# First expert place built by one-hot products from the residual tiles, router logits from unnormalised rows, router and experts in one block, room gathers issued at place 7

## The reference

```
x   = x + concat(NA, RWKV, MEM) @ W_out
x   = x + HierMoE(RMSNorm(x))

def rms_norm(x, w):
    y = xf * lax.rsqrt(jnp.mean(xf * xf, axis=-1, keepdims=True) + RMS_EPS)
    return y * w
def hierarchical_moe(h, ...):
    glogits = h2 @ w_group + b_group            # 4 groups, argmax
    elogits = h2 @ w_expert + b_expert          # 16 experts, top 2 inside the group
    ... weights = g_w[:, None] * top_p
    # for every expert: its tokens' rows xb = h2[toks]
    hid = jax.nn.silu(xb @ w_gate[e]) * (xb @ w_up[e])
    out = (hid @ w_down[e]) * wts[:, None]      # added to the token's row
```

## Time and profile before

| | us |
|---|---|
| median of 3 runs | 1241.48 (1239.05 to 1243.29) |
| the profiled execution | 1245.58 |
| its span in the trace | 1243.9 |
| PE busy in the span | 1159.4 |
| DVE busy | 558.1 |
| ACT busy | 307.5 |
| POOL busy | 213.7 |
| mean granted TensorE clock | 0.971 of full speed |

### The profile page before, as it was taken

How to read it: one execution, slowest core, us unless ns; L and a number is a source line. 1 busy time by engine, 2 the same in 40 slices (tenths; PEclk the granted TensorE clock), 3 DMA queues, 4 the chain that set the end, 5 groups by cost and what they waited for, 6 DMA issues and landing times. The chain is left out here.

```text
span 1243.9 us, 24829 instructions
## 1 busy us (share of the span) xinstructions
PE 1159.4 (93%) x10130; PEld 654.0 (53%) x10130; DVE 558.1 (45%) x1345; ACT 307.5 (25%) x791; POOL 213.7 (17%) x260
## 2 busy tenths in 40 slices
PE   5999999999999888899999999749999999899996
PEld 5534444444444566699995455524444444455553
DVE  4448536899695554555773344634111111111111
ACT  5154114432220666633441222200000000000000
POOL 0200410110000324200000001241345511112211
PEclk9989999999999899999999999869999999999998
DMA  9311422151301833234424831557999989667433
GB/s 325 98 42 39 156 79 67 34 177 48 113 17 53 188 77 109 71 86 115 125 58 170 323 120 69 199 230 286 366 359 339 379 326 368 229 254 279 135 123 108
DMA packets 104988, 209.57 MB, mean 168 GB/s; under 512 B 35509, under 2 KB 70805, under 8 KB 100777
## 3 DMA queue, kind: packets, MB, share of 16 engines
q1 hardware_dynamic: 79688, 129.28, 30.2%
q0 software_dynamic: 17264, 47.22, 11.4%
q10 hardware_dynamic: 7920, 31.46, 7.5%
HBM read 178.75 MB, written 35.58 MB: 172 GB/s over the span
## 5 line engine op out<-in xcount | busy, mean ns | idle before, releaser
L522 PE MATMUL pj_ps<-hT,pj_w 128*128 128x512 f32 x576 | 254.1, 597 | 0.0
L522 PEld LDWEIGHTS pj_ps<-hT,pj_w 128*128 128x128 f32 x576 | 108.3, 191 | 136.0 <-issue 135.5
L2197 PE MATMUL ex_py<-wd,ex_hT 128*128 128x512 f32 x256 | 115.2, 601 | 0.0
L1404 PE MATMUL ps_out<-w_out,mixT 128*128 128x512 f32 x256 | 112.3, 594 | 2.1 <-PEq L2571 1.8
L2452 DVE TENSOR_TENSOR ex_hid<-ex_pu,ex_sg 128x512 f32<-128x512 f32 x16 | 11.1, 692 | 193.8 <-PE ex_pu L2259 189.9
L2249 PE MATMUL ex_pg<-proj 128*128 128x512 f32 x176 | 79.3, 604 | 1.3 <-DVE proj L2389 1.3
L732 DVE RECIPROCAL mixT<-mixT 128x1024 f32<-128x1024 f32 (+1 forms) x11 | 68.9, 6262 | 24.2 <-ACT mixT L652 19.2
L1404 PEld LDWEIGHTS ps_out<-w_out,mixT 128*128 128x128 f32 x256 | 47.8, 190 | 59.5 <-issue 59.4
L2259 PE MATMUL ex_pu<-proj 128*128 128x512 f32 x176 | 77.3, 592 | 0.0
L2342 ACT ACTIVATE ex_sg<-ex_pg 128x512 f32<-128x512 f32 x16 | 9.6, 597 | 270.9 <-PE ex_pg L2249 270.9
L2197 PEld LDWEIGHTS ex_py<-wd,ex_hT 128*128 128x128 f32 x256 | 47.8, 194 | 53.7 <-issue 53.7
(11 more groups left out here) (363 smaller groups left out, 1947.9 us busy)
## 6 DMA issues: line engine op xcount, KB each, us to landing
wd<-in_moe_w_down ACTq DMA_DIRECT2D x15, 2048.0 KB, 9.8
proj<-in_moe_w_gate SPq DMA_DIRECT2D x11, 2048.0 KB, 10.3
proj<-in_moe_w_up SPq DMA_DIRECT2D x11, 2048.0 KB, 10.4
mixT<-in_moe_w_gate SPq DMA_DIRECT2D x5, 2048.0 KB, 9.3
mixT<-in_moe_w_up SPq DMA_DIRECT2D x5, 2048.0 KB
pj_w<-in_w_in SPq DMA_DIRECT2D x18, 512.0 KB, 4.0
proj<-in_x SPq DMA_DIRECT2D x16, 512.0 KB, 10.8
products<-pj_unit POOLq DMA_DIRECT2D x4, 2048.0 KB, 9.7
```

Source lines behind the costliest of these rows:

```text
L522: mm = pe.matmul(ps[:, t % 2, half, :], w_tile(t)[:, n, :], s.hT[:, n, half * 512:(half + 1) * 512], start=(n == 0), stop=(n == KD - 1))
L1404: mm = pe.matmul(s.ps_out[:, t % 2, half * 512:(half + 1) * 512], s.mixT[:, k, t * P:(t + 1) * P], s.w_out[:, k, half * 512:(half + 1) * 5 ...
L2197: mm = pe.matmul(py[:, half, :], hT[:, j, :], wd[e % 2][:, j, half * 512:(half + 1) * 512], start=(j == 0), stop=(j == KF - 1))
```

## The change

- **Router.** `turn` transposes x1 itself, not `h`; the norm weight is folded into the router weights once (`folded`), and 1/rms (`rate`) is applied where the bias is added. The router weights are loaded in another layout, and one more small load brings the norm weight (`w_turned`).
- **First place.** For each tile DVE makes a one-hot matrix `pick` (slot number equal to 0..127, times `rate`), and `collect` multiplies each of the 8 chunks of x1 by it, over all 8 tiles, into one PSUM buffer: 64 products of 128x128. The result is the transposed and gathered input of place 0; `copy_first` scales it by the norm weight into xT. The gather, transpose and copy of place 0 are gone. In a `collect` the stationary operand is `interleaved(s.x1[:, t, :], KD)[:, k, :]`, read at a step of 8 elements (32 bytes).
- **Order in the router's end.** DVE's `norm` of the last tile is split and its second half moved behind `place`; `order_experts` now stands behind `copy_first`; ACT's Exp of pair 2 comes before the last square and root.
- **One block.** The barrier and the second block are gone; small tensors of the router stay allocated.
- **Rooms.** POOL issues the first two room gathers at place 7; PE's `turn_room` stands in the middle of the up products, and DVE's `copy_rows` ahead of the hidden product.

```diff
@@ router stage @@
-            sp.dma_start(wr[:, :, 0:NG], s.inp["moe_w_group"].rearrange("(p k) n -> p k n", p=P)).then_inc(router_in, 16)
+            sp.dma_start(wr[:, :, 0:NG], s.inp["moe_w_group"].rearrange("(k p) n -> p k n", p=P)).then_inc(router_in, 16)
...
+            sp.dma_start(s.w_turned, s.inp["ffn_norm_w"].rearrange("o (p k) -> p (o k)", p=P)).then_inc(router_in, 16)
...
                 for part in range(2):
-                    pe.wait_ge(normed, 2 * q + part + 1)
+                    pe.wait_ge(added, 2 * q + part + 1)
                     for k in HALF_K[part]:
-                        mm = pe.transpose(pt[:, k, :], h[:, q % 2, k * P:(k + 1) * P], s.ident)
+                        mm = pe.transpose(pt[:, k, :], s.x1[:, q, k * P:(k + 1) * P], s.ident)
                     mm.then_inc(turned, 1)
...
+            def collect(t, chunks):
+                pe.wait_ge(selected, t // 2 + 1)
+                for k in chunks:
+                    mm = pe.matmul(s.ps_out[:, 0, k * P:(k + 1) * P], interleaved(s.x1[:, t, :], KD)[:, k, :], pick[:, t, :],
+                                   start=(t == 0 and k % 4 == 0), stop=(t == TT - 1 and k % 4 == 3))
+                return mm
...
             turn(TT - 1)
+            pe.wait_ge(added, 2 * (TT - 1))
+            collect(0, HALF_K[0])
             logits_of(TT - 1)
+            collect(0, HALF_K[1])
+            for t in (1, 2):
+                collect(t, range(KD))
             ranks(PAIRS - 1)
+            for t in range(3, TT - 2):
+                collect(t, range(KD))
+            for part in range(2):
+                collect(TT - 2, HALF_K[part])
+                collect(TT - 1, HALF_K[part]).then_inc(gathered, 1)
...
+                link(dve.tensor_tensor(nearest[:, two], slotf[:, 0, two], slotf[:, 1, two], ALU.min))
+                dve.wait_ge(inverted, 2 * g + 2)
+                for t in (2 * g, 2 * g + 1):
+                    ins = dve.tensor_scalar(pick[:, t, :], places, nearest[:, t:t + 1], rate[:, t:t + 1], ALU.is_equal, ALU.mult)
+                ins.then_inc(selected, 1)
+                dve.tensor_copy(slot[:, :, two], slotf[:, :, two]).then_inc(placed, 1)
...
-                dve.tensor_tensor(lg[:, q, :], pl[:, 0, 0:NG + NE], br[:, :], ALU.add).then_inc(biased, 1)
+                dve.scalar_tensor_tensor(out=lg[:, q, :], in0=pl[:, 0, 0:NG + NE], scalar=rate[:, q:q + 1], in1=br[:, :], op0=ALU.mult, op1=ALU.add).then_inc(biased, 1)
+
+            def copy_first(half):
+                dve.wait_ge(gathered, half + 1)
+                k = slice(HALF_K[half][0], HALF_K[half][-1] + 1)
+                dve.tensor_tensor(s.xT[:, 0, k, :], s.ps_out[:, 0, half * 512:(half + 1) * 512].rearrange("p (k t) -> p k t", t=P),
+                                  b3(s.w_turned[:, k].unsqueeze(2), [P, KD // 2, P]), ALU.mult).then_inc(s.first_copied, 1)
...
             choose_pair(PAIRS - 2)
+            weigh(PAIRS - 2)
             add(TT - 1, 1)
-            norm(TT - 1)
+            place(PAIRS - 2)
             bias(TT - 2)
-            weigh(PAIRS - 2)
-            place(PAIRS - 2)
+            invert(TT - 1)
+            norm(TT - 1, 0)
             bias(TT - 1)
             choose_pair(PAIRS - 1)
             weigh(PAIRS - 1)
             place(PAIRS - 1)
+            norm(TT - 1, 1)
+            copy_first(0)
+            copy_first(1)
             order_experts()
...
             copy(TT - 2)
+            exponents(PAIRS - 2)
             square(TT - 1)
-            exponents(PAIRS - 2)
             copy(TT - 1)
@@ expert stage @@
-        nc.all_engine_barrier()
-        block = c.enter_context(nc.Block())
+        block = s.stage
...
             sp.wait_ge(s.out_in, 16 * TT)
+            sp.wait_ge(s.first_copied, 2)
...
-            for e in range(2):
-                expert_rows(s, pool, e)
+            expert_rows(s, pool, 1)
...
-                if e == FIRST_ROOM - 1:
+                if e == SORTED - 1:
                     pool.wait_ge(zeroed, 2)
                     pool.wait_ge(room_in, 16 * sum(P // n for n in ROOM_ROWS))
                     for q in range(2):
...
-            turn_x(0)
             for e in range(NE):
...
                 for j in range(KD):
+                    if e == 0 and j % (KD // 2) == 0:
+                        pe.wait_ge(s.first_copied, 2 * j // KD + 1)
                     mm = pe.matmul(pg[:, :], xT[:, u, j, :], wg[g][:, j, :], start=(j == 0), stop=(j == KD - 1))
...
                 for j in range(KD):
+                    if e >= FIRST_ROOM and j == KD // 2:
+                        turn_room(e - FIRST_ROOM)
                     mm = pe.matmul(pu[:, :], xT[:, u, j, :], wu[g][:, j, :], start=(j == 0), stop=(j == KD - 1))
                 mm.then_inc(upped, 1)
-                if e >= FIRST_ROOM:
-                    turn_room(e - FIRST_ROOM)
-                else:
+                if e < FIRST_ROOM:
                     turn_x(e + 1)
...
             for e in range(NE):
                 q = e - FIRST_ROOM
+                if q >= 0:
+                    dve.wait_ge(xo_turned, q + 1)
+                    copy_rows()
                 dve.wait_ge(silu, e + 1)
...
-                if q >= 0:
-                    dve.wait_ge(xo_turned, q + 1)
-                    copy_rows()
-                else:
+                if q < 0:
                     copy_x(e + 1)
```

More of the change, by code:

```diff
@@ L1529, in out_projection_router @@
         wr = s.proj[:, C_ALL - 1, 0:KD * (NG + NE)].rearrange("p (k n) -> p k n", k=KD)
-        br = sb("br", [P, NG + NE])
-        st = sb("st", [P, 2, 4])
-        lg = sb("lg", [P, TT, NG + NE])
-        gmax, gmin, den, m1, m2, e2v = (sb(n, [P, 2]) for n in ("gmax", "gmin", "den", "m1", "m2", "e2"))
-        t4, t4b, goh, sel = (sb(n, [P, 2, 4]) for n in ("t4", "t4b", "goh", "sel"))
-        t44 = sb("t44", [P, 2, 4, 4])
-        eoh = sb("eoh", [P, 2, 2, 4])
-        both = sb("both", [P, 2, NE])
-        rank = sb("rank", [P, 2, NE])
-        t16 = sb("t16", [P, 2, 2, NE])
-        slotf = sb("slotf", [P, 2, 2])
+        spare = s.proj[:, C_ALL - 1, 160:512]
+        s.w_turned, rate, nearest = (spare[:, n * KD:(n + 1) * KD] for n in range(3))
+        slotf = spare[:, 32:48].rearrange("p (k t) -> p k t", k=2)
+        places = spare[:, 48:48 + P]
+        pick = s.expert_x[:, 0, :].rearrange("p (t n) -> p t n", t=TT)
+        br, st, lg, gmax, gmin, den, m1, m2, e2v = (s.op[n] for n in ("br", "st", "lg", "gmax", "gmin", "den", "m1", "m2", "e2"))
+        t4, t4b, goh, sel, t44, eoh, both, rank, t16 = (s.op[n] for n in ("t4", "t4b", "goh", "sel", "t44", "eoh", "both", "rank", "t16"))
+        unused, entry, wt, slot = (s.op[n] for n in ("unused", "entry", "wt", "slot"))
         room = s.proj[:, C_ALL - 1, 512:1024]
@@ L1609, in logits_of @@
                 if q == 0:
-                    pe.wait_ge(router_in, 80)
+                    pe.wait_ge(folded, 1)
                 if q:
@@ L1770, in _ @@
             link(dve.memset(s.count[:, :], 0.0))
+            link(dve.tensor_copy(places[:, 0:P // 2], s.iota))
+            link(dve.tensor_scalar(places[:, P // 2:P], s.iota, float(P // 2), None, ALU.add))
             def add(t, half):
@@ L1802, in _ @@
                 add(t, 1)
-                norm(t)
+                invert(t)
+                norm(t, 0)
+                norm(t, 1)
+                if t == 0:
+                    dve.tensor_tensor(wr, wr, b3(s.par("ffn_w", KD).unsqueeze(2), [P, KD, NG + NE]), ALU.mult).then_inc(folded, 1)
                 if t >= 2:
@@ L2385, in copy_x @@
             def copy_x(e):
-                dve.wait_ge(x_turned, e + 1)
+                dve.wait_ge(x_turned, e)
                 if e >= 2:
@@ L2578, in hybrid_layer @@
                                      for name, k in (("wg_in", GU_SETS), ("wu_in", GU_SETS), ("wd_in", 2)))
-        with c_mix:
-            s.ps_out = c_mix.enter_context(nc.psum_tensor("ps_out", [P, 2, D], F32))
-            rwkv_out(nc, s)
-            out_projection_router(nc, s)
-        experts(nc, s)
+        with ExitStack() as s.stage_sems:
+            with c_mix:
+                s.ps_out = c_mix.enter_context(nc.psum_tensor("ps_out", [P, 2, D], F32))
+                rwkv_out(nc, s)
+                s.stage = s.stage_sems.enter_context(nc.Block())
+                out_projection_router(nc, s)
+            experts(nc, s)
 def constants(np):
```

69 lines of the change are left out of this document (39 added, 30 removed).

## The result

The changed kernel takes 1231.24 us (median of 5 runs, 1228.88 to 1232.53), the kernel before 1241.86 beside it (5 runs, 1239.05 to 1244.34): a recorded ratio of 0.9903, interval 0.9881 to 0.9925 (the two medians alone give 0.9914). By the medians that is 10.6 us faster where 16.6 were forecast. The profiled execution took 1229.47, span 1227.8. Its span is 16.1 shorter than that of the kernel before, but 6.2 of it lie ahead of the router's block, in code that both share (its first output product starts at 679.36 and at 685.54); the stretch that was changed is 9.9 shorter.

What follows compares the result with a forecast made beforehand. PE, busy 93% of the span, was taken as the bound, with holes at the router-expert seam and place 11. Gains 1.0 + 4.2 + 8.4 + 3.0 = 16.6 us gave 1229.0 profiled, 1224.9 against the median; own range 1220 to 1230, wider 1210 to 1235.

Steps and rivals of the forecast that it cites:

- the seam: Between router and experts, where PE waited for place 0's gather: filling it with collect and other work gains 4.2 us.
- Router's start: Tile 0's transposes need only x1 and no longer wait for DVE's norm: gain 1.0 us.
- What p is: Spacing of one collect pass: taken as 0.213 us, doubled for the 32-byte step as in DVE's norm; bounds 0.106 and 0.32.
- 31.5 - 128p: Seam's gain up to place 1's gate, with 5.0 us other PE work before place 0's gate and 15.9 between gates.
- Rival 1: The step costs PE nothing: p = 0.109, seam gains 16.7 after short waits of 0.3 and 0.5, time 1212.4; chance 0.29.
- Rival 3: Clock not held: collect runs at 1.2 GHz, p = 0.43, total loss about 15 us, time 1256; chance 0.05.
- granted clock 1.00 from 793 to the first gate: Sign to look for in the seam: PE keeps the full clock through collect.
- Rival 4: Room gathers gain nothing, another transfer being late at place 11: 8.2 of 16.6 us left, time 1233.3; chance 0.04.
- All covered, the gather by 6 us: After the later expert order, place 2's weights and row gather still arrive in time; the gather lands at 850.4, transposes about 856.
- Room gathers: Issued at place 7, some 75 us before PE wants them, they end the wait at place 11: gain 8.4 us, clock included.
- Room copies: At places 12 to 15 four up products cover PE's wait for copy_rows: 4 x 0.76 = 3.0 us.
- The dropped barrier: Removing it between router and experts gives nothing by itself, since each queue waits for the order's tables anyway.

Runs made afterwards that it cites:

- contig: Changed kernel with collect reading elements side by side (step of one), place 0's input columns in another order; 0.9839 of the kernel before.
- kp: Changed kernel with place 0's gate and up weights loaded in another layout, so collect reads contiguous elements and the whole computation is kept; 0.9842 of the kernel before.
- after_again: The changed kernel run once more, unedited, on another chip; 0.9912 of the kernel before.
- The four kernels of the last set: Run on another chip: changed kernel again (0.9912), with place 3's gather issued early (0.9906), with collect at 16 and 8 bytes (1225.84, 1226.68 us).
- the seven of the first two sets: The kernels with the rooms' edit among the first eight, run on one chip; 0.9757 to 0.9911 of the kernel before.
- step2: Changed kernel with collect reading every second element (8 bytes apart), place 0's input columns in another order; 1226.68 us, one execution.
- rooms_only: Kernel before with only the rooms' half: room gathers at place 7, transposes in the up products, room copies first; 0.9911 of the kernel before.
- step4: Changed kernel with collect reading every fourth element (16 bytes apart), place 0's input columns in another order; 1225.84 us, one execution.
- kp_early3: kp with place 3's gather issued as soon as its buffer is free, ahead of the second row read and 12 table loads; 0.9791 of the kernel before.

## Why the prediction was right and where it was not

The sign was right and the time lies in the range, though 1.2 us above the forecast's own (to 1230). The sign rests on the rooms' half alone, where the mechanism came as forecast and the size nearly (11.0 for 11.4); the first place's half was forecast at 5.2 and paid nothing. The forecast gain was 6 us too high, most of it in the first place's half. By the traces (9.9 us gained where 16.6 were forecast): the seam is short by 4.0, place 3 by 1.6, the rooms by 1.3.

- *Router's start, 1.0.* From the first output product of the router's block to the end of the last (679.36 to 786.15; before 685.54 to 793.57) 106.79 us instead of 108.03: 1.2. The size holds.
- *The seam, 4.2 forecast, 0.2 measured.* The step that failed is "What p is". Its formula holds: 31.5 - 128p with p = 0.240 is 0.8, and the other work took 0.4 more than the 5.0 and 0.2 more than the 15.9. But p = 0.213 was 0.027 short, which 128 passes make 3.4 us: it doubled 0.1065, where a contiguous pass takes 0.113, and the factor is 0.240/0.113 = 2.1, where DVE's rows gave 1.9. Each makes about half of the 3.4. Choosing the strided row over the contiguous one was right. The place where load and stream overlap was argued rightly too: p is far below 0.32.
- *Rivals.* Rival 1 (no price for the step) fell: p is 0.240 with the step and 0.113 without. Its two short waits, 0.3 and 0.5, came in contig as 0.27 and 0.31. Its time would not have come even at that spacing: contig and kp gained 1.6% on the kernel before, some 19.6 us, not the 29.1 of the rival, since place 3's rows were late. Of rival 3 the clock came and the price did not: from 793 to 799 the granted clock was 0.50 with PE busy throughout, against the sign "granted clock 1.00 from 793 to the first gate", but a pass stayed at 0.240 and not 0.43. Only the 16 logits that the fall reached were slower: 1.98 us from 791.12 to 793.10, and 1.70 in after_again, where the clock was still 1.00 at that place. That is 0.28 of the 0.4 above. From 803 to the gate the clock was 1.00. Rival 4 fell: the room gathers gave their 8.4.
- *"All covered, the gather by 6 us"* was wrong, by one gather. The check ended at place 2. Its gather was covered, as said; the order came 42.1 us behind the router's last output product, before 23.3 (828.27 - 786.15, and 816.87 - 793.57), 18.8 later where 15.6 were forecast. But behind it in POOL's queue stood two row reads, 12 table loads of about 1.15 us each, and the gather of place 3, released together with 8 MB of weights. The bound of 13.9 for a landing came from a kernel in which the gather went out 1 us ahead of the gate and the weights were spread over 22 us; here it took 27.1. Cost 1.6 us in the profiled execution, 0.05 to 2.5 over three.
- *Room gathers, 8.4.* Measured 8.5, by the mechanism named: no wait at place 11, and down in 6.87.
- *Room copies, 3.0.* A place now lasts 0.85 less, 4 x 0.85 = 3.4. In the changed kernel's execution 1.0 was lost at place 12, where the room's up products break off after 12 passes (the row at 1112.72). The four kernels of the last set show the same loss (1.0 to 1.2), the seven of the first two sets with the rooms' edit do not. step2 has it and contig has not, and they differ only in the elements that `collect` reads; so by one execution of each it goes with the set, which ran on another chip, and not with the code. What makes it wasn't found. From the gate of place 3 on, the seven gain 10.9 to 11.3 us (rooms_only 12.2) against 11.4 forecast.
- *The dropped barrier, nothing.* From the last write's issue to the end are 8.0 to 8.5 us in kernels whose router and experts are one block (8.27 in the changed one), 7.5 in the one before and 7.1 in rooms_only. So the changed kernel loses 0.8 us at the very end. The kernels split by one block or two, but nothing was tried there, so the cause isn't shown.

## What to carry to other kernels

To fill a hole with work is worth the hole less that work, and the work's own spacing decides: measure or bound the access step of the stationary operand first, and if a layout of some weights can be chosen so that the step is at most 8 bytes (fp32, the case measured), choose it. When an early stage gets faster or a decision moves behind a copy, follow every queue that the decision releases down to its last entry of the first few stages, not only to the first one. A gather's landing time read in one kernel holds only for the load on the DMA engines at which it was issued. And two kernels' times can differ by several us in code that they share: compare the changed stretch by its own start and end.

## What the runs showed of the hardware

- The fp32 weight load of 128x128 jumps with its element distance between 8 and 16 bytes: 192 and 196 ns at 4 and 8 bytes, 329 and 336 at 16 and 32. The pass spacing follows, 0.113, 0.119, 0.234, 0.240 us; at 32 bytes it was the same at a granted clock of 0.50 and of 1.00.
- The granted clock fell to 0.50 with PE busy throughout while it ran passes at 32 bytes (6 us in the changed kernel, 793 to 799) and at 16 (step4); at 4 and 8 bytes it stayed at 1.00 in the same stretch (contig, kp, step2).
- With the DMA engines full (share 1.01 and 417 GB/s from 836 to 900), a gather of 512 KB took 27.1 us behind 12 small table loads in its queue, and 31.9 in kp; with place 3's ahead of them no gather of kp_early3 took over 22.8, the middle one 11.1. In the kernel before the same 12 loads stood ahead of it and it took 8.4 us, with the weights issued over 22 us instead of 5; the weights' own share is not shown by a run.
- ScalarE copied four blocks of 128x128 from PSUM with a scale for each partition in 1.14 us, where VectorE's one instruction for the same half took 0.69; it was free there, and that decided.
